# Finding the experts' indices by an exclusive or and a minimum instead of compare, multiply and sum

## The chip, the cores and the metric

The kernel runs on one core of a Trainium2 chip. The metric is the device time of one execution in microseconds (us), as the median of several runs. The core's engines are TensorE (PE in the profile, its weight loads PEld), VectorE (DVE), ScalarE (ACT), GpSimd (POOL) and SyncE (SP). Each works through a queue of its own in order; semaphores tie the queues together.

## The reference, cut to what matters

The whole computation is a block with two feed-forward layers and a mixer, and then two "hybrid" layers, each followed by a layer of many small experts (`peer_ffn`). For each of 256 tokens and 8 heads, that layer scores two lists of 128 keys, keeps the 16 best of each, adds them to 256 pairs, keeps the 16 best pairs, and needs the number of the expert behind each kept pair:

```python
def peer_ffn(x, w_query, sub_keys, down, up):
    q = (xt @ w_query).reshape(T, H, 2, PEER_HALF)
    s = jnp.einsum('thcd,cnd->thcn', q, sub_keys).astype(jnp.float32)
    sv, si = lax.top_k(s, K)                                    # K = 16, values and indices
    cand_s = (sv[:, :, 0, :, None] + sv[:, :, 1, None, :]).reshape(T, H, K * K)
    cand_i = (si[:, :, 0, :, None] * PEER_NKEYS + si[:, :, 1, None, :]).reshape(T, H, K * K)
    top_s, pos = lax.top_k(cand_s, K)                           # pos = 16 a + b
    idx = jnp.take_along_axis(cand_i, pos, axis=-1)             # the look-up
    gate = jax.nn.softmax(top_s, axis=-1)
    ...                                                         # sum of gate * gelu(down[idx] . x) * up[idx]
```

The change is in the look-up: from pos = 16 a + b to the a-th index of the first list and the b-th of the second.

## The kernel before, in words

Everything is a stream of weight tiles of 128x1024 float32, 512 KB each. A product in near float32 precision is made of three fast ones (`mm3`, L607 to L609): each weight tile is split into a high part (ScalarE, L1213) and a low part (the tile less its high part: VectorE, L1846, or GpSimd, L2720). There are four buffers for tiles as loaded and three for the parts, so the high part of tile k waits for TensorE to be through with tile k - 3, and TensorE waits for the low part of tile k before tile k. `LOWS` says which engine makes the low part. In an expert layer, with its tiles counted from 0, tiles 11 to 72 go three times to GpSimd and then once to VectorE: VectorE's are tiles 14, 18, 22, ..., 34, ..., 58, 62, 66, 70.

In an expert layer 8 tiles give the queries, 128 the scores of all 16384 experts (`down`), and 128 the sum (`up`). The kernel computes all experts and multiplies by gates that are zero except for the found ones. While tiles 8 to 67 are multiplied, VectorE searches beside its low parts. `BESIDE` spreads this `search` over 60 steps, one behind each tile, 30 for each half of the tokens (t = 0, 1). Each engine has a generator of its own; one `yield` is one step. Counted within a half (step 0 is at tile 8, or at tile 38), VectorE does: steps 1 to 11 the 16 best of each list (`best_of_keys`); step 12 the sum of pairs `cand` (L2564) and the conversion of the found indices to float, `sif` (L2567); steps 13 to 20 the 16 best pairs (L2575 to L2589); step 20, too, the shift, the mask and two conversions that give a and b (L2594 to L2599), and then the look-up of a half c = 0: compare (L2608, a 128x2048 one-hot of a against 0 to 15), step 21 multiply by the indices (L2612), step 22 sum over sixteen (L2615); steps 23 to 25 the same for c = 1; then the difference from the best (L2620), and after ScalarE's exponential (L1740) the gates (L2624 to L2628). TensorE turns the result at step 29 (L1159), and the one-hots of the next phase wait for it.

All eight PSUM banks are given out by `take` and `give` as a ring: the bank freed earliest is taken next, and TensorE waits in its queue for the event under which it was given. A pair of score tiles takes one bank, the keys' product (L1146) one, the turned result one.

Of the kernel before, what the change touches and what calls it, by code (L numbers as in the profile page):

```python
# [8 lines left out]
ALU = mybir.AluOpType  # L9
AX = mybir.AxisListType  # L10
F32 = mybir.dt.float32
F32R = mybir.dt.float32r
U32 = mybir.dt.uint32
# [338 lines left out]
def peer_memory(M, stage):  # L352
    m = Place()
    m.C = M.tensor(M.work_at, 128 * T).rearrange("p (n t) -> p n t", n=128)
    hole, M.hole = M.hole, None
    M.begin(M.work_at + 128 * T)
    m.keep = M.get3(3, T)
    m.temp = M.get3(2, T)
    m.waiting = [M.get3(8, 32) for _ in range(2)]
    M.hole = hole  # L360
    M.begin(M.work_at + 64 * T)
    m.qT, m.sk = M.get3(8, T), M.get(256)
    m.ws = [M.get(128) for _ in range(4)]
    m.sv, m.si, m.tv, m.pos = M.get(256), M.get(256), M.get(128), M.get(128)
    m.cand, m.eq, m.other = M.get(2048), M.get(2048), M.get(2048)
    m.sif, m.ab, m.out3 = M.get(256), M.get3(2, 128), M.get3(3, 128)
    assert M.at <= M.work_at + 128 * T
    M.hole = None
    M.begin(M.x_at)
    m.o1 = [M.get3(4, 128) for _ in range(2)]  # L370
    m.o2 = [M.get3(4, 128) for _ in range(2)]
    M.begin(M.x_at)
    m.his, m.los = [M.get3(4, T)], [M.get3(4, T)]
    M.begin(M.fixed_h)
    for ring in (m.his, m.los):
        ring += [M.get3(4, T) for _ in range(2)]
    M.hole = hole
    return m
# [208 lines left out]
class Tensor(Lane):  # L587
# [549 lines left out]
    def search(self):  # L1137
        M, m, e, s = self.M, self.m, self.e, self.s
        for t in range(2):
            for g in range(4):  # L1140
                bank = self.take()
                self.K.bank["keys", s, t, g] = bank
                self.wait_ge("peer_q", s, 3)
                self.wait_ge("sk_in", s)
                for i in range(2):
                    x = e.matmul(bank[:, 256 * i:256 * (i + 1)], m.qT[:, 2 * g + i, 128 * t:128 * (t + 1)], m.sk,  # L1146
                                 start=True, stop=True)
                x.then_inc(*self.S.tick("keys", s, t, g))
                yield
                yield  # L1150
                yield
                self.give(bank, ("keys_read", s, t, 2 * g + 1))
            for _ in range(17):
                yield
            bank = self.take()
            self.K.bank["found", s, t] = bank
            self.wait_ge("found", s, t, 2)
            for j in range(3):
                x = e.transpose(bank[:, 128 * j:128 * (j + 1)], m.out3[:, j], M.const("ident"))  # L1159
            x.then_inc(*self.S.tick("found_turned", s, t))  # L1160
            self.give(bank, ("kept", s, t))
            yield
# [674 lines left out]
class Vector(Lane):  # L1837
# [712 lines left out]

    def search(self):
        M, m, e, s = self.M, self.m, self.e, self.s
        iota16 = M.const("iota")[:, 0:16]
        e8, r8 = M.tiny(self.name, "e8", 8), M.tiny(self.name, "r8", 8)
        for t in range(2):
            for h in range(8):
                if h % 2 == 0:
                    yield
                self.best_of_keys(t, h)
                yield  # L2560
            s4 = m.sv.rearrange("p (h c k) -> p h c k", c=2, k=16)
            self.settle()
            self.wait_ge("keys_read", s, t, 7)
            e.tensor_tensor(m.cand.rearrange("p (h a b) -> p h a b", h=8, a=16),  # L2564
                            s4[:, :, 0].unsqueeze(3).to_broadcast([128, 8, 16, 16]),
                            s4[:, :, 1].unsqueeze(2).to_broadcast([128, 8, 16, 16]), ALU.add).then_inc(*self.mark())
            e.tensor_copy(m.sif, m.si.bitcast(U32)).then_inc(*self.mark())  # L2567
            yield
            for h0 in range(0, 8, 2):
                cs = [m.cand[:, 256 * h:256 * (h + 1)] for h in (h0, h0 + 1)]  # L2570
                v = [m.tv[:, 16 * h:16 * h + 16] for h in (h0, h0 + 1)]
                p = [m.pos[:, 16 * h:16 * h + 16].bitcast(U32) for h in (h0, h0 + 1)]
                self.settle()
                for i in range(2):
                    e.max(v[i][:, 0:8], cs[i]).then_inc(*self.mark())  # L2575
                first = self.n_own - 1
                for i in range(2):
                    self.settle(first + i)
                    e.max_index(p[i][:, 0:8], v[i][:, 0:8], cs[i]).then_inc(*self.mark())
                for i in range(2):  # L2580
                    self.settle(first + 2 + i)
                    e.match_replace(cs[i], v[i][:, 0:8], cs[i], TAKEN).then_inc(*self.mark())
                yield
                for i in range(2):
                    self.settle(first + 4 + i)
                    e.max(v[i][:, 8:16], cs[i]).then_inc(*self.mark())
                for i in range(2):
                    self.settle(first + 6 + i)
                    e.max_index(p[i][:, 8:16], v[i][:, 8:16], cs[i]).then_inc(*self.mark())  # L2589
                if h0 < 6:  # L2590
                    yield
            au, bu = m.eq[:, 0:128].bitcast(U32), m.eq[:, 128:256].bitcast(U32)
            self.settle()
            e.tensor_scalar(au, m.pos.bitcast(U32), 4, None, op0=ALU.logical_shift_right).then_inc(*self.mark())  # L2594
            e.tensor_scalar(bu, m.pos.bitcast(U32), 15, None, op0=ALU.bitwise_and).then_inc(*self.mark())
            self.settle(self.n_own - 1)
            e.tensor_copy(m.ab[:, 0], au).then_inc(*self.mark())
            self.settle(self.n_own - 1)
            e.tensor_copy(m.ab[:, 1], bu).then_inc(*self.mark())  # L2599
            s4f = m.sif.rearrange("p (h c k) -> p h c k", c=2, k=16)  # L2600
            if t:
                self.wait_ge("found_turned", s, 0)
            for c in range(2):
                buf = (m.eq, m.other)[c]
                b3 = buf.rearrange("p (k a) -> p k a", a=16)
                b4 = buf.rearrange("p (h k a) -> p h k a", h=8, a=16)
                self.settle()
                e.tensor_tensor(b3, iota16.unsqueeze(1).to_broadcast([128, 128, 16]),  # L2608
                                m.ab[:, c].unsqueeze(2).to_broadcast([128, 128, 16]), ALU.is_equal).then_inc(*self.mark())
                yield  # L2610
                self.settle()
                e.tensor_tensor(b4, b4, s4f[:, :, c].unsqueeze(2).to_broadcast([128, 8, 16, 16]), ALU.mult).then_inc(*self.mark())  # L2612
                yield
                self.settle()
                e.tensor_reduce(m.out3[:, 1 + c], b3, AX.X, ALU.add).then_inc(*self.S.tick("found", s, t, c))  # L2615
                if c == 0:
                    yield
            tv3 = m.tv.rearrange("p (h k) -> p h k", h=8)
            g3 = m.out3[:, 0].rearrange("p (h k) -> p h k", h=8)
            e.tensor_tensor(g3, tv3, tv3[:, :, 0:1].to_broadcast([128, 8, 16]), ALU.subtract).then_inc(*self.S.tick("best", s, t))  # L2620
            yield
            yield
            self.wait_ge("best_exp", s, t)
            e.tensor_reduce(e8, g3, AX.X, ALU.add).then_inc(*self.mark())  # L2624
            self.settle()
            e.reciprocal(r8, e8).then_inc(*self.mark())
            self.settle()
            e.tensor_tensor(g3, g3, r8.unsqueeze(2).to_broadcast([128, 8, 16]), ALU.mult).then_inc(*self.S.tick("found", s, t, 2))  # L2628
            yield
            yield  # L2630
            yield
# [609 lines left out]
```

## Time and profile before

| | us |
|---|---|
| median of 3 runs | 2531.29 |
| lowest, highest | 2525.47, 2531.94 |
| the profiled execution | 2531.54 |
| its span, first to last instruction | 2529.7 |
| TensorE busy | 2439.4 (96%) |
| VectorE busy | 1675.0 (66%) |
| ScalarE busy | 1204.4 (48%) |
| GpSimd busy | 711.8 (28%) |

Time in the rows below runs from the start of the span. "Busy" is the time in which an engine works on an instruction, or for VectorE and GpSimd also waits inside one for an access that it needs. The granted clock (PEclk) is the share of TensorE's full speed in a stretch; it has two levels, 1.2 and 2.4 GHz. Matmuls overlap, so the distance between two of them, which the chain of waits shows, says more than the length of one.

### The profile page before, as it was taken

What the parts mean: (1) busy time and instruction counts of PE and PEld (TensorE: products, weight loads), DVE (VectorE), ACT (ScalarE), POOL (GpSimd) and SP (SyncE); (2) the same over time, 40 slices, a digit from 0 to 9 for tenths busy, and PEclk for the clock granted to TensorE, in tenths of its full rate; (3) what the DMA queues carried; (4) which work ended last, traced back from release to release, by engine and by line L of the source; (5) the groups of instructions that cost most, each with busy time, mean ns of one, the idle gap of its engine ahead of it and who ended that gap; (6) DMA issues with size and microseconds to landing.
All of it is one profiled execution on the core that took longest, in us unless ns stands there. A gap on an engine that the chain in (4) does not pass through costs nothing.

```text
span 2529.7 us, 40330 instructions
## 1 busy us (share of the span) xinstructions
PE 2439.4 (96%) x16347; PEld 2233.2 (88%) x16347; DVE 1675.0 (66%) x3111; ACT 1204.4 (48%) x1827; POOL 711.8 (28%) x333
## 2 busy tenths in 40 slices
PE   4999899999999999999999999999999999999999
PEld 3997878988889999999888888889999999888887
DVE  6887775546565787899544445664877899644444
ACT  4444665445654444443444445654444444444443
POOL 3111001112025661000344443115663000244443
PEclk9999999999999999999999999999999999999999
DMA  7988444665345554444565665335554444555554
GB/s 282 327 300 308 162 138 151 216 195 171 109 159 170 169 166 154 139 142 142 191 196 192 194 193 194 127 125 186 165 177 157 137 140 142 181 192 193 193 192 165
DMA packets 126589, 457.45 MB, mean 181 GB/s; under 512 B 13974, under 2 KB 16962, under 8 KB 125635
## 3 DMA queue, kind: packets, MB, share of 16 engines
q1 hardware_dynamic: 121442, 441.52, 52.4%
q10 hardware_dynamic: 4048, 8.91, 1.0%
q0 software_dynamic: 912, 4.42, 0.5%
q8 instruction: 130, 2.13, 0.3%
q14 instruction: 57, 0.46, 0.1%
HBM read 451.62 MB, written 5.93 MB: 181 GB/s over the span
## 4 chain that ended last, share of the span: by engine, by line
PE 79%; DVE 6%; ACT 1%; issue 0%; POOL 0%; ACTq 0%; DVEq 0%; POOLq 0%
PE bank L607 24%; PE bank L609 23%; PE bank L608 23%; PE bank L1170 4%; DVE sb L2612 1%; DVE sb L2608 1%; DVE sb L1846 1%; PE bank L955 1%; PE bank L1146 1%; PE bank L816 0%; ACT sb L1213 0%; DVE sb L2615 0%; PE bank L622 0%; PE bank L1098 0%; PE bank L973 0%
## 5 line engine op out<-in xcount | busy, mean ns | idle before, releaser
L607 PE MATMUL bank<-sb,sb 128*128 128x256 f32 (+1 forms) x4744 | 1523.1, 321 | 49.1 <-DVE sb L1846 37.0
L608 PE MATMUL bank<-sb,sb 128*128 128x256 f32 (+1 forms) x4744 | 1497.3, 316 | 0.0
L609 PE MATMUL bank<-sb,sb 128*128 128x256 f32 (+1 forms) x4744 | 1497.2, 316 | 0.0
L1213 ACT ACTIVATE sb<-sb 128x1024 fp32r<-128x1024 f32 x765 | 806.6, 1058 | 1087.1 <-PE bank L609 1079.7
L2720 POOL TENSOR_TENSOR sb<-sb,sb 128x1024 fp32r<-128x1024 f32 x256 | 644.1, 2519 | 1337.6 <-ACT sb L1213 1333.6
L607 PEld LDWEIGHTS bank<-sb,sb 128*128 128x128 f32 x4744 | 911.5, 192 | 118.8 <-issue 35.4
L1846 DVE TENSOR_TENSOR sb<-sb,sb 128x1024 fp32r<-128x1024 f32 x509 | 626.2, 1231 | 559.6 <-ACT sb L1213 558.3
L608 PEld LDWEIGHTS bank<-sb,sb 128*128 128x128 f32 x4744 | 911.9, 192 | 55.2 <-issue 1.0
L609 PEld LDWEIGHTS bank<-sb,sb 128*128 128x128 f32 x4744 | 911.0, 192 | 55.4
L2684 DVE TENSOR_TENSOR sb<-sb,sb 128x1024 fp32r<-128x1024 f32 x64 | 160.0, 2499 | 149.7 <-ACT sb L1802 149.7
L2647 DVE TENSOR_SCALAR sb<-sb,sb 128x128 f32<-128x128 f32 x512 | 142.2, 341 | 0.0
L1170 PE MATMUL bank<-sb,sb 128*128 128x128 f32 x1024 | 135.3, 275 | 0.4 <-DVE sb L2647 0.4
L1170 PEld LDWEIGHTS bank<-sb,sb 128*128 128x128 f32 x1024 | 125.7, 192 | 0.7 <-issue 0.7
L1861 DVE CUSTOM_DVE_ANT_0 sb<-sb,sb 128x1024 f32<-128x1024 f32 x68 | 96.5, 1428 | 10.4 <-ACT sb L1219 5.8
L2643 DVE TENSOR_TENSOR sb<-sb,sb 128x512 f32<-128x512 f32 x128 | 87.3, 682 | 0.0
L2743 POOL TENSOR_TENSOR sb<-sb,sb 128x1 f32<-128x1 f32 (+2 forms) x28 | 18.6, 666 | 233.9 <-DVE sb L1882 101.0
L1802 ACT ACTIVATE sb<-sb 128x1024 fp32r<-128x1024 f32 x64 | 66.9, 1045 | 10.1 <-DVE sb L2679 5.1
L2658 DVE TENSOR_TENSOR sb<-bank,sb 128x288 f32<-128x288 f32 (+7 forms) x128 | 68.1, 534 | 0.0
L1362 ACT ACTIVATE sb<-sb 128x256 fp32r<-128x256 f32 x44 | 18.4, 418 | 102.4 <-DVE sb L2085 102.4
L622 PE MATMUL bank<-sb,sb 128*128 128x128 f32 x152 | 29.5, 336 | 32.0 <-DVE sb L1899 30.1
L622 PEld LDWEIGHTS bank<-sb,sb 128*128 128x128 f32 x152 | 21.4, 168 | 42.1 <-issue 28.4
L1780 ACT ACTIVATE sb<-bank 128x512 f32<-128x512 f32 (+7 forms) x120 | 57.7, 481 | 0.1
(274 smaller groups left out, 1238.7 us busy)
## 6 DMA issues: line engine op xcount, KB each, us to landing
sb<-in_peer_down_dram SPq DMA_DIRECT2D x256, 512.0 KB, 3.3
sb<-in_peer_up_dram SPq DMA_DIRECT2D x256, 512.0 KB, 3.3
sb<-in_w_ada_dram SPq DMA_DIRECT2D x72, 512.0 KB, 6.5
sb<-in_hyb_in_dram SPq DMA_DIRECT2D x56, 512.0 KB, 3.4
sb<-in_ffn_gate_dram SPq DMA_DIRECT2D x44, 512.0 KB, 4.3
sb<-in_ffn_up_dram SPq DMA_DIRECT2D x44, 512.0 KB, 5.2
sb<-in_ffn_down_dram SPq DMA_DIRECT2D x44, 512.0 KB, 4.3
sb<-in_mix_in_dram SPq DMA_DIRECT2D x25, 512.0 KB, 4.1
```

The source lines that it names most:

```text
L607: e.matmul(out, a[0], b[0], start=start, stop=False)
L608: e.matmul(out, a[0], b[1], start=False, stop=False)
L609: return e.matmul(out, a[1], b[0], start=False, stop=stop)
L1170: x = self.e.matmul(bank[:, 128 * j:128 * (j + 1)], m.o2[g % 2][:, j], m.o1[g % 2][:, j], start=True, stop=True)
L1213: self.e.activation(rr(M.hi[k % NSPLIT]), M.raw[k % NRAW], AF.Copy).then_inc(*self.S.tick("hi", k))
L1846: self.e.tensor_tensor(rr(M.lo[k % NSPLIT]), M.raw[k % NRAW], M.hi[k % NSPLIT], ALU.subtract).then_inc(*self.S.tick("lo_dve", k))
L1861: self.e.tensor_tensor_reduce(w, w, M.sc, 1.0, 0.0, ALU.mult, ALU.add, M.mod[:, o:o + 1]).then_inc(*self.S.tick("ada_dve", n))
L2643: e.tensor_tensor(o2, iota, m.keep[:, 2, 4 * g:4 * g + 4].unsqueeze(2).to_broadcast(wide), ALU.is_equal).then_inc(*self.S.tick("one_hot2", ...
L2647: x = e.tensor_scalar(o1[:, j], M.const("iota"), m.keep[:, 1, t:t + 1], m.keep[:, 0, t:t + 1], op0=ALU.is_equal, op1=ALU.mult)
L2658: e.tensor_tensor(c[:, 0:k], bank[:, 0:k], c[:, 0:k], ALU.mult).then_inc(*self.S.tick("gates_put", s, g))
L2684: self.e.tensor_tensor(rr(flat(m.los[i])), flat(m.C[:, 4 * n:4 * n + 4]), flat(m.his[i]), ALU.subtract).then_inc(*self.S.tick("up_lo", s, n))
L2720: self.e.tensor_tensor(rr(M.lo[k % NSPLIT]), M.raw[k % NRAW], M.hi[k % NSPLIT], ALU.subtract).then_inc(*self.S.tick("lo_pool", k))
```

## The change

Instead of a one-hot that is multiplied by the indices and summed, the kernel makes a table of 256 a + (the a-th index) as whole numbers. The found place gives 256 a of the pair wanted. An exclusive or of the two leaves the index alone where the a's agree, and something of at least 256 elsewhere; the smallest of the sixteen is the index. TensorE writes a (0 to 15, repeated for 8 heads and 2 lists) into a bank by a product with the identity, and VectorE multiplies by 256 and adds the indices within the bank. The number of steps stays 30 for each half of the tokens; the second minimum is at step 23, one step is empty, and the difference from the best stays at step 25.

```diff
@@ peer_memory
-    m.cand, m.eq, m.other = M.get(2048), M.get(2048), M.get(2048)
-    m.sif, m.ab, m.out3 = M.get(256), M.get3(2, 128), M.get3(3, 128)
+    m.cand = M.get(2048)
+    m.chosen = [M.get(2048).bitcast(U32) for _ in range(2)]
+    m.place, m.out3 = M.get3(2, 128).bitcast(U32), M.get3(3, 128)
@@ Tensor.search, after the four key products of a half (step 12)
+            bank = self.take()
+            self.K.bank["table", s, t] = bank
+            e.matmul(bank[:, 0:256], M.const("ident"), M.const("iota")[:, 0:16].unsqueeze(1).to_broadcast([128, 16, 16]),
+                     start=True, stop=True).then_inc(*self.S.tick("table", s, t))
+            self.give(bank, ("chosen", s, t, 1))
@@ Vector.search
-            e.tensor_copy(m.sif, m.si.bitcast(U32)).then_inc(*self.mark())
+            table = self.K.bank["table", s, t][:, 0:256]
+            self.wait_ge("table", s, t)
+            e.scalar_tensor_tensor(table.bitcast(U32), table, 256.0, m.si.bitcast(U32), ALU.mult, ALU.add).then_inc(*self.mark())
...
-            au, bu = m.eq[:, 0:128].bitcast(U32), m.eq[:, 128:256].bitcast(U32)
             self.settle()
-            e.tensor_scalar(au, m.pos.bitcast(U32), 4, None, op0=ALU.logical_shift_right).then_inc(*self.mark())
-            e.tensor_scalar(bu, m.pos.bitcast(U32), 15, None, op0=ALU.bitwise_and).then_inc(*self.mark())
-            self.settle(self.n_own - 1)
-            e.tensor_copy(m.ab[:, 0], au).then_inc(*self.mark())
-            self.settle(self.n_own - 1)
-            e.tensor_copy(m.ab[:, 1], bu).then_inc(*self.mark())
-            s4f = m.sif.rearrange("p (h c k) -> p h c k", c=2, k=16)
+            for c in range(2):
+                e.tensor_scalar(m.place[:, c], m.pos.bitcast(U32), (240, 15)[c], (4, 8)[c], op0=ALU.bitwise_and,
+                                op1=ALU.logical_shift_left).then_inc(*self.mark())
+            t4 = table.bitcast(U32).rearrange("p (h c a) -> p h c a", c=2, a=16)
             if t:
                 self.wait_ge("found_turned", s, 0)
             for c in range(2):
-                buf = (m.eq, m.other)[c]
-                b3 = buf.rearrange("p (k a) -> p k a", a=16)
-                b4 = buf.rearrange("p (h k a) -> p h k a", h=8, a=16)
                 self.settle()
-                e.tensor_tensor(b3, iota16.unsqueeze(1).to_broadcast([128, 128, 16]),
-                                m.ab[:, c].unsqueeze(2).to_broadcast([128, 128, 16]), ALU.is_equal).then_inc(*self.mark())
+                e.tensor_tensor(m.chosen[c].rearrange("p (h k a) -> p h k a", h=8, a=16),
+                                t4[:, :, c].unsqueeze(2).to_broadcast([128, 8, 16, 16]),
+                                m.place[:, c].rearrange("p (h k) -> p h k", h=8).unsqueeze(3).to_broadcast([128, 8, 16, 16]),
+                                ALU.bitwise_xor).then_inc(*self.S.tick("chosen", s, t, c))
                 yield
-                self.settle()
-                e.tensor_tensor(b4, b4, s4f[:, :, c].unsqueeze(2).to_broadcast([128, 8, 16, 16]), ALU.mult).then_inc(*self.mark())
+                self.wait_ge("chosen", s, t, c)
+                e.tensor_reduce(m.out3[:, 1 + c], m.chosen[c].rearrange("p (k a) -> p k a", a=16), AX.X, ALU.min).then_inc(
+                    *self.S.tick("found", s, t, c))
                 yield
-                self.settle()
-                e.tensor_reduce(m.out3[:, 1 + c], b3, AX.X, ALU.add).then_inc(*self.S.tick("found", s, t, c))
-                if c == 0:
-                    yield
+            yield
```

## Rows read from the trace of the kernel before

**Rows 1.** The page: busy time of each engine; the chain's shares.

```profile
PE 2439.4 (96%) x16347; PEld 2233.2 (88%) x16347; DVE 1675.0 (66%) x3111; ACT 1204.4 (48%) x1827; POOL 711.8 (28%) x333
...
PE 79%; DVE 6%; ACT 1%; issue 0%; POOL 0%; ACTq 0%; DVEq 0%; POOLq 0%
```

**Rows 2.** Busy time by stage: PE, PEld, DVE, ACT, POOL, clock, DMA share, GB/s.

```profile
760.00:970.00 210.00, 203.45 (x1644) 202.08 (x1643) 149.09 (x441) 94.08 (x109) 126.51 (x50) 0.98 0.51 168
```

**Rows 3.** TensorE's waits in the two search stretches: total us, times, longest us.

```profile
PE bank L607 <- DVE sb L1846: 6.5, 2, 4.2
...
PE bank L607 <- DVE sb L1846: 6.4, 2, 4.2
PE bank L1159 <- DVE sb L2628: 0.5, 1, 0.5
```

**Rows 4.** The chain that ended last around the first wait: start us, us, what.

```profile
835.84 0.14 DVE sb L2599
...
836.00 4.51 DVE sb L2608
...
840.54 4.39 DVE sb L2612
...
844.95 2.29 DVE sb L2615
847.24 1.14 DVE sb L1846
...
848.52 0.36 PE bank L607
...
849.53 0.21 PE bank L607
...
852.89 0.12 PE bank L608
```

**Rows 5.** The timeline of TensorE at the second and third wait.

```profile
950.59 0.36 PE L607 MATMUL bank<-sb,sb 128*128 128x256 f32 x1 [4.17 <-DVE sb L1846]
...
1815.92 0.36 PE L607 MATMUL bank<-sb,sb 128*128 128x256 f32 x1 [2.29 <-DVE sb L1846]
```

**Rows 6.** TensorE in stretches behind three waits: length, busy (count), granted clock, DMA.

```profile
850.00:852.00 2.00, 2.00 (x11) 0.50 1.01 403
1816.00:1820.00 4.00, 4.00 (x34) 1.00 0.81 288
1916.00:1920.00 4.00, 2.52 (x12) 0.71 0.35 123
```

**Rows 7.** The timeline of VectorE: the conversion, and a compare without GpSimd.

```profile
902.86 2.49 DVE L2567 CAST sb<-sb 128x256 f32<-128x256 uint32 x1
...
930.18 2.29 DVE L2608 TENSOR_TENSOR sb<-sb,sb 128x2048 f32<-128x2048 f32 x1
```

**Rows 8.** The timeline of GpSimd around the first wait.

```profile
835.96 2.40 POOL L2720 TENSOR_TENSOR sb<-sb,sb 128x1024 fp32r<-128x1024 f32 x1 [0.48 <-ACT sb L1213]
838.84 3.94 POOL L2720 TENSOR_TENSOR sb<-sb,sb 128x1024 fp32r<-128x1024 f32 x1 [0.48 <-ACT sb L1213]
```

**Rows 9.** VectorE's groups by form, mean ns of one: an operand in a bank.

```profile
L2658 DVE TENSOR_TENSOR sb<-bank,sb 128x480 f32<-128x480 f32 x16 | 10.1, 651 | 0.0
...
L2658 DVE TENSOR_TENSOR sb<-bank,sb 128x256 f32<-128x256 f32 x16 | 6.7, 418 | 0.0
```

**Rows 10.** The timelines of VectorE and GpSimd in the same time.

```profile
743.92 3.22 DVE L1948 SCALAR_TENSOR_TENSOR sb<-bank,sb,sb 128x256 fp32r<-128x256 f32 x8
...
742.95 5.66 POOL L2720 TENSOR_TENSOR sb<-sb,sb 128x1024 fp32r<-128x1024 f32 x2 [1.00 <-DVE sb L1899]
```

**Rows 11.** The timeline of ScalarE: two high parts that VectorE's low parts need.

```profile
840.58 1.06 ACT L1213 ACTIVATE sb<-sb 128x1024 fp32r<-128x1024 f32 x1 [1.82 <-PE bank L609]
...
940.44 1.06 ACT L1213 ACTIVATE sb<-sb 128x1024 fp32r<-128x1024 f32 x1 [1.81 <-PE bank L609]
```

**Rows 12.** The chain at one pair of key products.

```profile
770.85 0.86 PE bank L1146 x4
```

More of the change, by code:

```diff
@@ L2552, in search @@
         M, m, e, s = self.M, self.m, self.e, self.s
-        iota16 = M.const("iota")[:, 0:16]
         e8, r8 = M.tiny(self.name, "e8", 8), M.tiny(self.name, "r8", 8)
```

## The prediction

> **What bounds the kernel now.** I read the page first. TensorE is busy for 96% of the span and VectorE for 66%, and the chain that ended last runs through TensorE for 79% and through VectorE for 6% [rows 1]. So VectorE's time counts only where TensorE stands still for it. The table by stage gives the two stretches in which the search runs, one in each layer: of 210.00 us TensorE is busy 203.45 and VectorE 149.09 in the first [rows 2]. TensorE's waits in these two stretches name the rest: 6.5 us in two waits in the first layer and 6.4 us in two in the second, all before L607, for the subtraction L1846 (VectorE's low half of a weight tile), and 0.5 us for L2628 [rows 3].
>
> The chain through the first of these waits shows who was late. VectorE runs the compare L2608 for 4.51 us, the multiply L2612 for 4.39 and the sum L2615 for 2.29, and only then the low half L1846 that stands behind them in its queue. TensorE starts again at 848.52, and from about 849.5 to 852.7 its products come every 0.21 us, then every 0.12 again [rows 4]. The other waits look alike: TensorE starts again at 950.59 after 4.17 us and at 1815.92 after 2.29 [rows 5], and the longest of the second layer is again 4.2 us [rows 3]. The granted clock is at the lower of its two levels (0.50, which is 1.2 GHz of 2.4) after the first, above it and so partly low after the fourth (0.71), and stays at 1.00 after the third [rows 6].
>
> Why do compare and multiply take twice their time? L2608 took 2.29 us where it met no GpSimd work [rows 7] and 4.51 where it did [rows 4]. At 835.96 GpSimd had just begun a subtraction of 2.40 us, L2608 came at 836.00 and ended at 840.5; the next GpSimd subtraction came at 838.84 and took 3.94 [rows 8]. The two engines take turns, each waiting for the other's whole instruction, when VectorE reads two operands from SBUF.
>
> **What the four stalls cost now.** A wait costs its idle time, 0.24 us for a first product of 0.36 instead of 0.12 [rows 4], and the slow stretch. From 849.53 to 852.89 there are 16 products of 0.21 in 3.36 us, which at 0.12 would take 1.9: with the one that is slow in part, 1.5 us lost. I take the same after the second and the fourth wait. Hence:
> - first layer, t = 0: 2.29 + 0.24 + 1.5 = 4.0
> - first layer, t = 1: 4.17 + 0.24 + 1.5 = 5.9
> - second layer, t = 0: 2.29 + 0.24 = 2.5, with no slow clock
> - second layer, t = 1: 4.2 + 0.24 + 1.5 = 5.9
> - the wait of L1159 for L2628: 0.5
>
> Together 18.8 us, which is the most that the change can return.
>
> **The change, part by part.** *The chain of the look-up.* The compare and the multiply of each half go, and one exclusive or of 2048 elements takes their place, one operand of it in PSUM. Operations of this kind with one operand in a bank: 128x480 takes 651 ns and 128x256 takes 418, so 1.04 ns an element and, at 2048, 0.65 + 1568 x 0.00104 = 2.28 us [rows 9]. Does it wait for GpSimd? L1948, which reads a bank and one SBUF tensor, ran eight times in 3.22 us from 743.92, inside two GpSimd subtractions that held from 742.95 to 748.6 [rows 10]. It didn't wait, so I take 2.3 us. The upper bound is 4.5, a compare that takes turns. The minimum of sixteen takes the sum's place, with one input of the same shape: 2.29 [rows 4]; its input is uint32, as it was not before, and I give it no other price. Two conversions fall away, 0.14 us each [rows 4].
>
> *Time line at t = 0, first layer.* The two instructions for the places stand where the shift and the mask stood, with their shapes, and I give them the same time. Without the two conversions the first exclusive or starts at 835.7 instead of 836.0 [rows 4]; then 2.3 + 2.3 + 2.3 for or, minimum, or: 842.6. The high half that L1846 needs is there at 840.58 + 1.06 = 841.6 [rows 11]. L1846 takes 1.14 [rows 4] and ends at 843.8. TensorE wants it at 848.52 - 2.29 = 846.2. Margin 2.3 us, and the stall is gone.
>
> *At t = 1.* The first low half comes after the place instructions and the first compare, which already met no GpSimd work: 930.18 + 2.29 = 932.4 [rows 7], and with 1.14 for L1846 933.5. Here nearly nothing changes, and no wait of TensorE stands there today. After it now: 933.5 + 2.3 + 2.3 + 2.3 = 940.4 for minimum, or, minimum. The high half is there at 940.44 + 1.06 = 941.5 [rows 11], so L1846 ends at 942.7; TensorE wants it at 950.59 - 4.17 = 946.4. Margin 3.7 us. What is late next here is the high half itself, which waits for TensorE's own tile three back and leaves this margin. The second layer has the same lengths, so both its stalls go, and with VectorE some 7 us earlier L1159 no longer waits.
>
> *The table product.* TensorE gets four more products of 128x256 in plain float32 (two layers, two halves). Two such products, the keys' L1146, took 0.86 us [rows 12], so 0.43 each and 1.7 in all, on the path because TensorE is never idle there. The stationary operand is another and the moving one repeats its words; the bounds are 0 (no reason for a gain) and 2 x 0.43 = 0.86 each, 3.4 in all.
>
> *The table's instruction on VectorE* replaces the conversion L2567, which takes 2.49 us on 256 elements because it waits for GpSimd [rows 7]. A bank operand at 256 elements takes 0.42 [rows 9], so VectorE is 2 us earlier at this step, four times, all covered by TensorE's work. It brings a wait for the table product, with the whole selection of the 16 best and the next low half queued behind it. At t = 0 VectorE is at this step at 814.5, five us after TensorE has passed. At t = 1 it is close: TensorE wants tile 66 at 946.4, so at 2.88 us a tile (24 products of 0.12) tile 50 ends at 946.4 - 15 x 2.88 = 903.2, the table is ready at about 903.7, and VectorE came to L2567 at 902.86 [rows 7]. That wait of 0.8 us eats a part of the 2 us just won, so it costs nothing.
>
> *The bank.* The table holds one of eight banks from step 12 until the second exclusive or. Banks are taken in turn, and the seventh take after it is the pair of tiles 34 and 35 (t = 0) or 64 and 65 (t = 1). At t = 0 the second or ends at 842.6, before tile 34 is wanted at 846.2; at t = 1 it ends at 938.1, and tile 64 starts at 946.4 - 2 x 2.88 = 940.6. Margin 2.6 us, no wait.
>
> **Sum.** 18.8 - 1.7 = 17.1 us. The profiled execution took 2531.5 us (span 2529.7), which is the median of the runs shown (2531.3) to 0.3. 2531.5 - 17.1 = 2514.4, against the median 2514.2; I say 2514.
>
> **A rule that speaks against it.** L2608 reads a word repeated sixteen times and a row of sixteen words, and ran at 1.12 ns an element [rows 7]. The Trainium skill, "Vector Engine (DVE) Microarchitecture Reference", section 5.2, says that a port keeps its full rate only for runs of two or more adjacent words, and gives 1.73 ns a column for an exclusive or one of whose sources hops at every element. By it the exclusive or, if a repeated word counted as a hop, would take 3.5 us (an estimate from that page). The trace doesn't agree for repeated words in a compare.
>
> **The rivals.** Let D be the time of the exclusive or. From the two time lines the t = 0 stall is 2(D - 3.5), and the low half at t = 1 is late by D - 3.6 (tile 62 is wanted at 946.4 - 4 x 2.88 = 934.9).
> - *Integer operands lose the 1.04 ns rate mildly*, D = 3.5, as it would where repeated words are slow. For it: no uint32 pair with a bank operand in the trace. Against it: [rows 7]. Each half stalls for a few tenths, which costs 0.3 + 0.24, with the slow clock up to 1.5 more: 2516 to 2521. Chance 5%.
> - *The exclusive or takes turns with GpSimd after all*, D = 4.4. Stalls of 1.9 at t = 0, 0.8 at t = 1 before tile 62, and 0.8 before tile 64, where TensorE waits for the bank; with 0.24 each and one or two slow stretches 6 us a layer, 12 in all: 2514.4 + 12 = 2526. Against it stands [rows 10]. Chance 6%.
> - *The clock doesn't come back*: TensorE is no longer idle but the slow stretches stay, 3 x 1.5 = 4.5 us: 2519. For it: the clock stayed high after the third stall, so idleness alone doesn't set it. Against it: the slow products begin within a us or so of a restart [rows 4]. Chance 5%.
> - *Slower.* The bitwise operation on 32-bit integers from PSUM needs several cycles an element. From D = 5.0 the stalls (3.0 at t = 0, 1.4 before tile 62, 1.5 before tile 64 for the bank, 0.24 each, two slow stretches: 9.6 a layer) and the table products exceed the 18.8 us of now; at 6.7 us, three times the rate of [rows 9], t = 0 stalls for 6.4, t = 1 for 3.1 and again 3.1, with clock some 17 a layer: 2514.4 + 34 = 2548. Nothing in the trace shows such an operation at such a rate. Chance 3%.
>
> **How the numbers follow.** The forecast, all stalls gone at 2514, gets 81%. Its own range is -2 (the clock after the fourth stall, the keys' stretch with less work before it) to +4 (the table product at 0.86, a stall left over of some tenths), plus what three runs of before differ, 6 us: 2508 to 2521. The second and the fourth of the cases lie in this, too; up to 2522 about 1 in 10 is left out. Faster by over 0.3% (7.6 us, about what a measurement of this kernel can tell from no change) means below 2523.7: 0.88. Within: 0.08, mainly the second rival. Slower: 0.04.
>
> **What would show it.** In the profile after: no wait of L607 for L1846 in the two search stretches, and none of L1159; the exclusive or x8 at 2.3 us with minimum, median and maximum alike; GpSimd's subtractions of 3.94 back at 2.40; the granted clock of both stretches at 1.00; four table products at 0.43. VectorE's busy time falls: eight compares and eight multiplies of 2.3 to 4.5 leave, eight of 2.3 come. A third of the gain missing with the clock low would show the third rival; a wait of L607 for ScalarE's Gelu or for the or itself would show that the bank is late. I am wrong if D is above 3.5.

## The result

| | before | after |
|---|---|---|
| median of 4 runs, us | 2531.09 | 2512.03 |
| lowest to highest | 2525.47 to 2531.94 | 2509.72 to 2513.0 |
| span of the profiled execution | 2529.7 | 2510.7 |
| TensorE's waits of L607 (L608 after) for VectorE's low half, whole span | 37.0 us, 18 times | 23.7 us, 14 times |

The ratio is 0.9928 with a 95% interval of 0.9916 to 0.9940: 19 us or 0.72% faster. Lines have moved by one to six: the three products are now L608 to L610, VectorE's low half L1852, ScalarE's high half L1219, the one-hots' product L1176; GpSimd's low half is still L2720.

The page of the changed kernel, busy time and the chain's shares, which answer to [rows 1]:

```profile
PE 2432.4 (97%) x16355; PEld 2228.2 (89%) x16355; DVE 1623.3 (65%) x3095; ACT 1206.1 (48%) x1827; POOL 697.0 (28%) x333
...
PE 83%; DVE 2%; ACT 1%; issue 0%; POOL 0%; ACTq 0%; POOLq 0%
```

VectorE's share of the chain fell from 6% to 2%, and its busy time by 52 us. Its share of the span was, as before, not the point. The table by stage (length; PE, PEld, DVE, ACT and POOL busy; clock, DMA share, GB/s), against [rows 2]:

```profile
770.00:960.00 190.00, 190.00 (x1558) 189.04 (x1557) 120.23 (x430) 89.80 (x103) 117.07 (x48) 1.00 0.54 174
1728.00:1917.00 189.00, 189.00 (x1551) 188.04 (x1550) 119.69 (x429) 89.80 (x103) 116.59 (x48) 1.00 0.54 174
```

In both search stretches TensorE is busy all the time and the granted clock is 1.00. The stretch of [rows 2] is 20 us longer; in 770 to 960 alone, the kernel before had TensorE busy for 183.45 us and VectorE for 142.69. The list of TensorE's waits in these stretches is empty, where [rows 3] had 6.5 and 6.4 us and the 0.5 us of L1159.

VectorE's timeline at the look-up of t = 0 in the first layer, against the chain of [rows 4]:

```profile
835.22 0.61 DVE L2601 TENSOR_SCALAR sb<-sb 128x128 uint32<-128x128 uint32 x2
835.87 2.29 DVE L2608 TENSOR_TENSOR sb<-bank,sb 128x2048 uint32<-128x2048 uint32 x1
838.20 2.29 DVE L2614 TENSOR_REDUCE sb<-sb 128x128 f32<-128x2048 uint32 x1
840.40 2.28 DVE L2608 TENSOR_TENSOR sb<-bank,sb 128x2048 uint32<-128x2048 uint32 x1
842.60 1.22 DVE L1852 TENSOR_TENSOR sb<-sb,sb 128x1024 fp32r<-128x1024 f32 x1
843.73 2.28 DVE L2614 TENSOR_REDUCE sb<-sb 128x128 f32<-128x2048 uint32 x1
```

And GpSimd's in the same time, against [rows 8]:

```profile
836.09 2.41 POOL L2720 TENSOR_TENSOR sb<-sb,sb 128x1024 fp32r<-128x1024 f32 x1 [0.47 <-ACT sb L1219]
838.97 2.41 POOL L2720 TENSOR_TENSOR sb<-sb,sb 128x1024 fp32r<-128x1024 f32 x1 [0.47 <-ACT sb L1219]
```

The second exclusive or starts at 840.40, while GpSimd is at work from 838.97 to 841.38, and takes 2.28 us. GpSimd's subtractions take 2.41 both times, where the second took 3.94, though the first exclusive or ran from 835.87 to 838.16. The low half starts at 842.60 instead of 847.24.

The instructions by line, for the exclusive or and for the table's instruction (durations in ns: shortest, median, longest):

```profile
L2608 DVE TENSOR_TENSOR sb<-bank,sb x8: 2280/2288/2293, 835.9 to 1889.6; 128x2048 uint32<-128x2048 uint32 x8
...
L2574 DVE SCALAR_TENSOR_TENSOR bank<-bank,sb x4: 420/426/433, 814.2 to 1857.1; 128x256 uint32<-128x256 f32 x4
...
  PE bank L1156: 0.9, 2
```

The exclusive or took 2280 to 2293 ns in all eight cases. The table's instruction took 0.42 us instead of 2.49, and had to wait for the table product in two of the four cases, 0.9 us together. One table product on the chain:

```profile
808.50 0.43 PE bank L1156 x2
```

A measure that leaves out the rest of the kernel is the time from the first key product to the first one-hots' product of a layer. The view of a single line gives the first and the last start (after the durations); for the two lines in the first layer of the changed kernel:

```profile
L1147 PE MATMUL bank<-sb,sb x32: 377/378/379, 770.4 to 890.0; 128*128 128x256 f32 x32
...
L1176 PE MATMUL bank<-sb,sb x512: 272/275/348, 960.1 to 1195.8; 128*128 128x128 f32 x171
```

Before, the lines were L1146 and L1170. The differences of the first starts:

| | first layer | second layer |
|---|---|---|
| before | 969.7 - 770.7 = 199.0 | 1936.7 - 1738.1 = 198.6 |
| after | 960.1 - 770.4 = 189.7 | 1917.7 - 1728.0 = 189.7 |

18.2 us of the 19.0 by which the spans differ are here. I call it the search time below.

### The profile page after: what moved, and what is told of

It reads as the page before. It is cut to its first block, busy times and chain, and to the rows that moved or that the text cites. A ratio compares the mean times of both kernels' runs of the same rounds, so it can differ in the third digit from the quotient of the medians.

```text
span 2510.7 us, 40330 instructions
## 1 busy us (share of the span) xinstructions
PE 2432.4 (97%) x16355; PEld 2228.2 (89%) x16355; DVE 1623.3 (65%) x3095; ACT 1206.1 (48%) x1827; POOL 697.0 (28%) x333
## 4 chain that ended last, share of the span: by engine, by line
PE 83%; DVE 2%; ACT 1%; issue 0%; POOL 0%; ACTq 0%; POOLq 0%
PE bank L608 25%; PE bank L609 25%; PE bank L610 25%; PE bank L1176 4%; PE bank L956 1%; PE bank L1147 1%; PE bank L817 1%; DVE sb L1852 0%; PE bank L1099 0%; PE bank L623 0%; PE bank L974 0%; POOL sb L2743 0%; DVE sb L1905 0%; PE bank L806 0%; PE bank L1061 0%
## 5 line engine op out<-in xcount | busy, mean ns | idle before, releaser
L608 PE MATMUL bank<-sb,sb 128*128 128x256 f32 (+1 forms) x4744 | 1520.5, 321 | 36.5 <-DVE sb L1852 23.7
L610 PE MATMUL bank<-sb,sb 128*128 128x256 f32 (+1 forms) x4744 | 1493.9, 315 | 0.0
L1219 ACT ACTIVATE sb<-sb 128x1024 fp32r<-128x1024 f32 x765 | 808.1, 1060 | 1085.2 <-PE bank L610 1077.2
L1852 DVE TENSOR_TENSOR sb<-sb,sb 128x1024 fp32r<-128x1024 f32 x509 | 625.2, 1229 | 585.1 <-ACT sb L1219 583.8
L608 PEld LDWEIGHTS bank<-sb,sb 128*128 128x128 f32 x4744 | 907.9, 191 | 104.6 <-issue 20.9
L2720 POOL TENSOR_TENSOR sb<-sb,sb 128x1024 fp32r<-128x1024 f32 x256 | 629.3, 2460 | 1336.6 <-ACT sb L1219 1332.6
L610 PEld LDWEIGHTS bank<-sb,sb 128*128 128x128 f32 x4744 | 907.8, 191 | 55.9
L1176 PE MATMUL bank<-sb,sb 128*128 128x128 f32 x1024 | 135.3, 275 | 0.4 <-DVE sb L2647 0.4
L1176 PEld LDWEIGHTS bank<-sb,sb 128*128 128x128 f32 x1024 | 125.7, 192 | 0.7 <-issue 0.7
```

Of the source, the lines that this page charges most:

```text
L608: e.matmul(out, a[0], b[0], start=start, stop=False)
L610: return e.matmul(out, a[1], b[0], start=False, stop=stop)
L1176: x = self.e.matmul(bank[:, 128 * j:128 * (j + 1)], m.o2[g % 2][:, j], m.o1[g % 2][:, j], start=True, stop=True)
L1219: self.e.activation(rr(M.hi[k % NSPLIT]), M.raw[k % NRAW], AF.Copy).then_inc(*self.S.tick("hi", k))
L1852: self.e.tensor_tensor(rr(M.lo[k % NSPLIT]), M.raw[k % NRAW], M.hi[k % NSPLIT], ALU.subtract).then_inc(*self.S.tick("lo_dve", k))
L2720: self.e.tensor_tensor(rr(M.lo[k % NSPLIT]), M.raw[k % NRAW], M.hi[k % NSPLIT], ALU.subtract).then_inc(*self.S.tick("lo_pool", k))
```

## The experiments

Is it that the operand left SBUF, or that one pass over 2048 elements fell away? Two kernels do one of the two alone.

**One operand in PSUM, all three passes kept.** The kernel before, with:

```diff
@@ Tensor.search, step 12: the table product of the change
@@ Vector.search
-            e.tensor_copy(m.sif, m.si.bitcast(U32)).then_inc(*self.mark())
...
+            e.tensor_copy(bank[:, 256:512], m.si.bitcast(U32)).then_inc(*self.mark())
...
-            s4f = m.sif.rearrange("p (h c k) -> p h c k", c=2, k=16)
+            s4f = bank[:, 256:512].rearrange("p (h c k) -> p h c k", c=2, k=16)
...
-                e.tensor_tensor(b3, iota16.unsqueeze(1)
...
+                e.tensor_tensor(b3, bank[:, 0:16].unsqueeze(1)
...
```

The bank is free again when the second multiply (c = 1) has read it, where the changed kernel frees it after the second exclusive or.

> The kernel before with its compare, multiply and sum kept; only one operand of the compare (0 to 15) and one of the multiply (the indices as floats) lie in a PSUM bank, written by the same table product and one conversion. Theory (the operand out of SBUF ends the turns with GpSimd): all three instructions take 2.29 us; at t = 0 the low half ends at 836.0 + 3 x 2.3 + 1.14 = 844.0 where TensorE wants it at 846.2, at t = 1 at 933.5 + 4 x 2.3 + 1.14 = 943.9 against 946.4. No wait of TensorE for the low half in either search, 2512 to 2514 us: the whole gain without one pass fewer. Rival (what counts is the pass that falls away): the stalls of 2.3 and 4.2 us stay, and the time is 2531 + 1.7 = 2533.

Measured: 2524.68 us, ratio 0.9979 (0.9969 to 0.9988), search time 198.0 in both layers. Neither theory had that. The traced execution is one of the slower of the ten (2528.81 us, where the lowest is 2522.46), so its search times show less of a gain than the median does; the last section says what these executions differ in. TensorE's waits in the first search (total us, times, longest):

```profile
PE bank L607 <- DVE sb L2618: 4.8, 2, 2.4
```

TensorE waits for L2618, the multiply, and not for the low half. VectorE's and TensorE's timelines around the first wait:

```profile
835.82 2.29 DVE L2614 TENSOR_TENSOR sb<-bank,sb 128x2048 f32<-128x2048 f32 x1
838.15 2.29 DVE L2618 TENSOR_TENSOR sb<-sb,bank 128x2048 f32<-128x2048 f32 x1
840.47 2.29 DVE L2621 TENSOR_REDUCE sb<-sb 128x128 f32<-128x2048 f32 x1
842.67 1.22 DVE L1851 TENSOR_TENSOR sb<-sb,sb 128x1024 fp32r<-128x1024 f32 x1
843.80 2.28 DVE L2614 TENSOR_TENSOR sb<-bank,sb 128x2048 f32<-128x2048 f32 x1
846.12 2.29 DVE L2618 TENSOR_TENSOR sb<-sb,bank 128x2048 f32<-128x2048 f32 x1
```

```profile
848.46 0.38 PE L607 MATMUL bank<-sb,sb 128*128 128x256 f32 x1 [2.41 <-DVE sb L2618]
```

Compare, multiply and sum take 2.29 us each and the low half of tile 34 is done at 843.8, as the theory had it (844.0). But TensorE wants the bank again at 846.05. The second multiply, which reads it last, ends at 848.4. The rule of the bank (the seventh take is tile 34) stands in the prediction, and I had not applied it to this kernel.

**The same, with the bank taken six steps later.**

```diff
@@ Tensor.search
+            for _ in range(6):
+                yield
             bank = self.take()
...
-            for _ in range(17):
+            for _ in range(11):
                 yield
@@ Vector.search: the conversion into the bank moved from step 12 to step 20
```

> As e1_psum_operands, but TensorE takes the bank and makes the table product six steps later, and VectorE converts the indices into it right before the first compare. Theory (in e1 the stalls of 2.4 us are not the look-up's length but the bank: TensorE wants it at tile 34 and 64, before the second multiply has read it): the seventh take now falls at tile 40 and 70, the two waits of 4.8 us in each search are gone, and the time is that of the changed kernel, 2512 to 2514, with compare, multiply and sum all kept. Rival (one pass fewer is what brings it): a wait of TensorE of 1 us or more stays in each half, 2518 or more.

Measured: 2513.30 us, ratio 0.9938 (0.9921 to 0.9955), search time 189.8 and 189.7, as in the changed kernel. TensorE waits for nothing in either search. TensorE in the first search stretch (length, busy, clock), then compare and multiply by line:

```profile
772.00:961.00 189.00, 189.00 (x1551) 1.00 0.53 174
...
L2616 DVE TENSOR_TENSOR sb<-bank,sb x8: 2282/2288/2292, 837.8 to 1894.2; 128x2048 f32<-128x2048 f32 x8
...
L2620 DVE TENSOR_TENSOR sb<-sb,bank x8: 2281/2286/2289, 840.1 to 1896.5; 128x2048 f32<-128x2048 f32 x8
```

So with all three passes kept, an operand in PSUM brings the whole gain. The fewer passes are not needed for it. What they do need is a bank that nobody wants early.

**The exclusive or with its table in SBUF.** The changed kernel, with:

```diff
-    m.place, m.out3 = M.get3(2, 128).bitcast(U32), M.get3(3, 128)
+    m.place, m.out3, m.table = M.get3(2, 128).bitcast(U32), M.get3(3, 128), M.get(256)
...
-            e.scalar_tensor_tensor(table.bitcast(U32), table, 256.0, m.si.bitcast(U32), ALU.mult, ALU.add).then_inc(*self.mark())
+            e.scalar_tensor_tensor(m.table.bitcast(U32), table, 256.0, m.si.bitcast(U32), ALU.mult, ALU.add).then_inc(*self.mark())
...
-            t4 = table.bitcast(U32).rearrange("p (h c a) -> p h c a", c=2, a=16)
+            t4 = m.table.bitcast(U32).rearrange("p (h c a) -> p h c a", c=2, a=16)
```

> The changed kernel, but the table of 256 a + index is written to SBUF, so the exclusive or reads two operands from SBUF. Theory (turns come back, but one pass fewer leaves room for them): the exclusive or takes 2.3 where it comes first and up to 4.5 where GpSimd does, and some of GpSimd's subtractions take about 4 instead of 2.4; at t = 0 the low half comes at 844 to 846.5 against 846.2, so TensorE waits for 0 to 0.5 us in each layer, 2512 to 2517 us. Rival (the turns alone made the stalls): an exclusive or of 4.4 each time, 6 us lost a layer, 2524. Rival (the turns have nothing to do with it): 2.3 each time and GpSimd at 2.40.

Measured: 2513.55 us, ratio 0.9935 (0.9920 to 0.9950), search time 191.5 and 191.6, 1.8 to 1.9 more than with the table in PSUM. TensorE's wait, then GpSimd's and VectorE's timelines:

```profile
PE bank L608 <- POOL sb L2720: 1.3, 1, 1.3
...
832.99 12.17 POOL L2720 TENSOR_TENSOR sb<-sb,sb 128x1024 fp32r<-128x1024 f32 x3 [0.48 <-ACT sb L1219]
...
832.77 2.29 DVE L2608 TENSOR_TENSOR sb<-sb,sb 128x2048 uint32<-128x2048 uint32 x1
...
839.50 3.39 DVE L1852 TENSOR_TENSOR sb<-sb,sb 128x1024 fp32r<-128x1024 f32 x1
```

The turns are back, and VectorE comes first: the exclusive or takes 2.29 us, the three subtractions of GpSimd take 12.17 together where 7.2 would do, and the low half of VectorE itself takes 3.39 instead of 1.22. TensorE waits 1.29 us, this time for GpSimd's low half. I had expected at most 0.5 us, and at VectorE's. So the shorter look-up with the turns back still brings 7.5 and 7.0 us of the 9.3 and 8.9. This holds for the order in which the two engines come here: the exclusive or took 2280 to 2322 ns in all eight cases, so it never had to wait for GpSimd to speak of, and in this one it came first by 0.22 us. The two conversions that fell away, 0.27 us together, are enough to give it this lead; in the kernel before, GpSimd was first by 0.04 us [rows 8]. What the exclusive or would cost where GpSimd comes first was not run.

**The table product four times** (three more `e.matmul` into the same bank before the one that is there).

> The changed kernel with the table product made four times instead of once, 12 products of 128x256 float32 more. Theory (each lies on TensorE's path at 0.43 us): +5.2 us on the changed kernel, 2517.2. Rival (a product is hidden somewhere): 2512. At the upper bound of 0.86 each it would be 2522.

Measured: 2516.67 us, ratio 0.9948 (0.9932 to 0.9963); search time 192.3 and 192.2, 2.6 and 2.5 more for six products: 0.43 each. The chain at one table:

```profile
808.02 1.30 PE bank L1157 x6
809.32 0.43 PE bank L1159 x2
```

1.73 us for four products. Each lies on the path at its full length.

**Without the table product.** VectorE writes the table from 0 to 15 and the indices, and waits itself for the bank:

```diff
@@ Tensor.search
-            bank = self.take()
-            e.matmul(bank[:, 0:256], M.const("ident"), M.const("iota")[:, 0:16].unsqueeze(1).to_broadcast([128, 16, 16]),
-                     start=True, stop=True).then_inc(*self.S.tick("table", s, t))
+            bank, self.K.bank["table_free", s, t] = self.free.pop(0)
             self.K.bank["table", s, t] = bank
@@ Vector.search
-            self.wait_ge("table", s, t)
-            e.scalar_tensor_tensor(table.bitcast(U32), table, 256.0, m.si.bitcast(U32), ALU.mult, ALU.add).then_inc(*self.mark())
+            for event in self.K.bank["table_free", s, t]:
+                self.wait_ge(*event)
+            e.scalar_tensor_tensor(table.bitcast(U32).rearrange("p (r a) -> p r a", a=16),
+                                   M.const("iota")[:, 0:16].unsqueeze(1).to_broadcast([128, 16, 16]), 256.0,
+                                   m.si.bitcast(U32).rearrange("p (r a) -> p r a", a=16), ALU.mult, ALU.add).then_inc(*self.mark())
```

> The changed kernel without the table product: VectorE writes the table into the bank itself from 0 to 15 and the indices, both in SBUF, and waits itself for the event under which the bank was freed. Theory: TensorE saves 4 x 0.43 = 1.7 us, VectorE's instruction takes 2.5 us where it meets GpSimd, as the conversion before the change did, and has room for it: 2510.3 us, no new wait of TensorE. Rival: the longer instruction or the earlier bank makes a low half late, 2512 or more.

Measured: 2509.84 us, ratio 0.9918 (0.9904 to 0.9931), search time 188.8 in both layers, 0.9 less each. The table's instruction by line:

```profile
L2573 DVE SCALAR_TENSOR_TENSOR bank<-sb,sb x4: 2630/2632/2632, 813.2 to 1854.2; 128x256 uint32<-128x256 f32 x4
```

It reads two operands from SBUF and takes 2.63 us each time, but has room. Since 2.2 us between two medians is less than these runs can tell, both kernels ran again, side by side on one chip.

> The changed kernel once more, unaltered, on the same chip as the next one, so that the two can be set side by side. Theory: 0.992 to 0.994 of the kernel before, no wait of TensorE of over 0.3 us in either search.

Measured: 2508.09 us, ratio 0.9916 (0.9902 to 0.9929), search time 189.7 and 189.7.

> The version without the table product again, beside the changed kernel. Theory: 1.7 us (0.07%) less than the changed kernel, four products of 0.43 us; the intervals of the two will overlap, and the spans between the first key product and the first gate product are the sharper measure: 0.9 us less in each layer. Rival: the 2.2 us seen between the medians was noise and VectorE's longer table instruction takes it back: no less.

Measured: 2511.87 us, ratio 0.9927 (0.9914 to 0.9941), search time 188.8 and 188.9. The order of the medians is the other way round. The 0.9 us is there in both layers of both pairs of traces; in the whole time it can't be told from noise, so this version is not shown to beat the changed kernel. Both beat the kernel before.

**The bank held too long.** The changed kernel with two more minima at t = 1, before the first one (step 21):

```diff
                 self.wait_ge("chosen", s, t, c)
+                for _ in range(2 if t == 1 and c == 0 else 0):
+                    e.tensor_reduce(m.ws[0], m.chosen[c].rearrange("p (k a) -> p k a", a=16), AX.X, ALU.min).then_inc(*self.mark())
+                    self.settle()
                 e.tensor_reduce(m.out3[:, 1 + c], ...)
```

> The changed kernel with two more minima of 2.29 us before the first one at t = 1 (step 21), so that the second exclusive or ends at 934.3 + 4.6 = 938.9, while TensorE wants tile 64 at 936.9. Theory (the bank is the seventh take): TensorE waits 2.1 us for the exclusive or itself in each layer, and the low half of tile 66, at 942.4, is in time for a TensorE that is now at 945; 2.1 + 0.24 and 0 or 1.5 of slow clock a layer: 5 to 8 us above the changed kernel. Rival (the bank is not wanted then): no such wait, and TensorE waits for nothing.

Measured: 2517.44 us in one run; search time 193.5 and 192.1, that is 3.8 and 2.4 more. TensorE's timeline at the wait:

```profile
937.76 0.39 PE L608 MATMUL bank<-sb,sb 128*128 128x256 f32 x1 [2.08 <-DVE sb L2608]
```

2.08 us for the exclusive or, once in each layer, 2.1 expected (the 1.4 between the layers is the clock, below), and no wait for the low half of tile 66. So the margin of the bank in the changed kernel is real: the exclusive or ends at 934.3 and TensorE takes the bank at 936.9.

**Two more minima at t = 0**, behind the second exclusive or (step 22).

```diff
                                 ALU.bitwise_xor).then_inc(*self.S.tick("chosen", s, t, c))
+                if c == 1 and t == 0:
+                    self.wait_ge("chosen", s, t, c)
+                    for _ in range(2):
+                        e.tensor_reduce(m.ws[0], m.chosen[c].rearrange("p (k a) -> p k a", a=16), AX.X, ALU.min).then_inc(*self.mark())
+                        self.settle()
```

> The changed kernel with two more minima behind the second exclusive or at t = 0 alone (step 22): the low half of tile 34 starts at 842.6 + 4.6 = 847.2 instead of 842.6 and is done at 848.5, and TensorE wants it at 846.2. Theory (a margin of 2.3 us): a wait for VectorE's low half of 2.2 to 2.4 us in each layer, as in the kernel before, and a loss of 2.5 to 4.0 a layer, 5 to 8 in all. Rival (a stall costs only its idle time): 4.6 in all.

Measured: 2518.85 us in one run; search time 192.3 and 192.4, that is 2.6 and 2.7 more than in the changed kernel. TensorE's timeline:

```profile
849.83 0.35 PE L608 MATMUL bank<-sb,sb 128*128 128x256 f32 x1 [2.36 <-DVE sb L1852]
```

2.36 us of waiting and 2.6 in all in a layer: as expected, at the lower end, since the clock stayed high.

**One more minimum in both halves** (the same, with `if c == 1` and `range(1)`).

> The changed kernel with one more minimum behind the second exclusive or in both halves (step 22): the low half of tile 34 is done at 846.2, just when TensorE wants it. Theory (margins of 2.3 us at t = 0 and over 3 at t = 1): waits of at most 0.2 us, time within 1 us of the changed kernel, 2512 to 2513. Rival (no such margin): waits of over 1 us and 4 us or more.

Measured: 2517.05 us in one run; search time 191.9 and 192.0. TensorE waits 1.97 us for the low half in each layer, where at most 0.2 us and a time of 2512 to 2513 us were expected. VectorE's and GpSimd's timelines:

```profile
842.78 2.29 DVE L2615 TENSOR_REDUCE sb<-sb 128x128 f32<-128x2048 uint32 x1
845.10 3.16 DVE L1852 TENSOR_TENSOR sb<-sb,sb 128x1024 fp32r<-128x1024 f32 x1
...
844.79 2.38 POOL L2725 TENSOR_TENSOR sb<-sb,sb 128x1024 fp32r<-128x1024 f32 x1 [3.35 <-ACT sb L1219]
```

The low half came at 845.10 and took 3.16 us instead of 1.22, because it reads two operands from SBUF and GpSimd had begun at 844.79. A margin of 2.3 us for its end was the wrong account: its start has to come before GpSimd's. In the changed kernel it starts at 842.60 and GpSimd at 844.73, so a delay of more than 2.1 us crosses this line and costs two at once.

## Why the prediction was right

2514 us was forecast and 2512.03 measured; the range was 2508 to 2522.

- *What bounds the kernel*: right. The four stalls before the low half and the one of L1159 are gone, and nothing took their place.
- *The time line at t = 0*: exclusive or at 835.7, ends at 838.0, 840.3 and 842.6 forecast; 835.87, and the next instructions at 838.20, 840.40 and 842.60 measured.
- *The time line at t = 1* is the forecast one, 3.8 us earlier, since TensorE comes earlier:

```profile
926.48 2.29 DVE L2608 TENSOR_TENSOR sb<-bank,sb 128x2048 uint32<-128x2048 uint32 x1
928.69 1.22 DVE L1852 TENSOR_TENSOR sb<-sb,sb 128x1024 fp32r<-128x1024 f32 x1
929.82 2.28 DVE L2614 TENSOR_REDUCE sb<-sb 128x128 f32<-128x2048 uint32 x1
932.02 2.28 DVE L2608 TENSOR_TENSOR sb<-bank,sb 128x2048 uint32<-128x2048 uint32 x1
934.33 2.29 DVE L2614 TENSOR_REDUCE sb<-sb 128x128 f32<-128x2048 uint32 x1
938.11 1.23 DVE L1852 TENSOR_TENSOR sb<-sb,sb 128x1024 fp32r<-128x1024 f32 x1 [1.49 <-ACT sb L1219]
```

  The low half waits for ScalarE there, which I had named as next late.
- *The exclusive or*: 2.28 from the slope over elements, 2.29 measured; that it doesn't wait for GpSimd was read from the one kind of instruction that had run beside it [rows 10]. The minimum over uint32 took 2.28.
- *The table product*: 0.43 each, shown by making it four times. *The table's instruction* had a wait of 0.8 us forecast at t = 1 in each layer; it was 0.45.
- *The bank*: no wait here, and two kernels that hold it for longer wait at just this take, so the count of seven takes was right.
- *The sum*: 17.1 us forecast, 19.1 between the medians, 19.0 between the spans, 18.2 in the two searches. For the first layer 9.9 - 0.86 = 9.0 was forecast and 9.3 came; for the second 8.9 - 0.86 = 8.0, and 8.9 came. The term that was sized too small is thus the loss in the second layer, by 0.9 us, and 18.8 us was not the most that the change could return: without the table products' 1.7, the two searches would have become 19.9 us shorter. The trace of the kernel before shows most of the rest. TensorE stood still briefly at three more places, once in the first layer and twice in the second:

```profile
940.44 0.35 PE L607 MATMUL bank<-sb,sb 128*128 128x256 f32 x1
...
1824.82 0.39 PE L607 MATMUL bank<-sb,sb 128*128 128x256 f32 x1
...
1907.34 0.35 PE L607 MATMUL bank<-sb,sb 128*128 128x256 f32 x1
```

  The products before these start at 940.07, 1824.51 and 1906.97, so 0.31 to 0.37 us lie between two products instead of 0.12, and up to 0.1 more behind each: some 0.3 us each time, 0.6 in the second layer. The profile names no releaser for so short a wait, but a GpSimd subtraction that took turns and ran for 4.49 us from 1820.28 ended at 1824.77, just before the second of them: the turns made GpSimd's low halves late, too. For L1159, 0.80 us lie between its start and that of the product before it, and I had given its wait 0.5 us and no restart: 0.2 more. The last 0.8 us lie outside the searches, where two traces of one kernel differ as much (2510.7 and 2509.8 us of the changed kernel, with equal search times).
- *The slow clock*: 4.5 us of the 18.8 are three slow stretches of one execution of the kernel before. By the last section the clock fell behind half of the waits of 2.0 to 2.4 us, so the two stalls of 2.29 us could have had two slow stretches, or none, in another execution. That one of each came, and an execution near the median, is luck in the hit.
- *The reason for the gain*: half right. The prediction put it to a look-up of two passes that doesn't take turns. The runs show that either alone brings all or most of the gain: three passes without turns give 189.7 to 189.8 us of search time, two passes with turns, in which VectorE came first, 191.5 and 191.6, both together 189.7. The prediction also tied the turns to two operands from SBUF, although its own row of the conversion L2567 has one and 2.49 us [rows 7].
- *The rivals*: none came, and the granted clock came back to 1.00 in both searches. The exclusive or keeps the rate of [rows 9] for whole numbers and for words repeated sixteen times. The rule of the Trainium skill ("Vector Engine (DVE) Microarchitecture Reference", section 5.2) on single hopping words does not reach to repeated ones here: 1.12 ns an element. But the rivals' prices were off: an exclusive or of 3.5 us would start the low half at 845.0, and by the run with one more minimum that costs about 2 us a layer, not 0.5. The threshold I gave was for the end of an instruction that itself has to take turns.

## What to carry to other kernels

Where VectorE and GpSimd both read two operands from SBUF, each waits for the whole of the other's instruction. One operand in PSUM ended that here: three passes without turns had a search time 1.7 to 1.9 us shorter than two with them. Two kinds of VectorE instruction behave otherwise. The conversion of 256 indices waited with only one operand, 2.49 us from SBUF to SBUF, and took 0.42 with its output in PSUM (the run with one operand in PSUM: at 813.89, with GpSimd at work from 812.73 to 818.61). The sum and the minimum over sixteen, which read one operand, took 2.27 to 2.29 us in all cases, also beside GpSimd. Count a held bank in takes, not in time: find which instruction takes it next and check that against the last reader, for every version. A margin in front of an instruction that takes turns ends where the other engine's next instruction starts, not where its own result is due.

## What the runs showed of the hardware

TensorE's clock after a wait of about 2 us is not set by the length of the wait alone. TensorE in stretches of 4 us behind four waits (length, busy, clock, DMA): first behind 2.41 us in the kernel with one operand in PSUM and the bank held,

```profile
849.00:853.00 4.00, 4.00 (x23) 0.59 0.53 181
```

then behind 2.36 us in the kernel with two more minima,

```profile
850.00:854.00 4.00, 4.00 (x35) 1.00 0.83 294
```

then behind the two waits of 2.08 us of one and the same execution of the kernel with the bank held too long, one in each layer:

```profile
938.00:942.00 4.00, 4.00 (x24) 0.61 0.29 113
1900.00:1904.00 4.00, 4.00 (x35) 1.00 0.21 57
```

Over all traces with a wait of 1.97 to 2.41 us in the searches the clock fell to its lower level behind 6 of 12 (before 1 of 2, three passes with the bank held 4 of 4, bank late 1 of 2, one more 0 of 2, two more 0 of 2). Behind 4.2 us it fell in 2 of 2, behind 1.3 us in 0 of 2. Where it fell (0.50 in between, 1.2 GHz), 4 us held 23 or 24 products instead of 35 or 36, so it costs about 1.5 us. What decides in between is open. Whole executions of one kernel differ in the clock, too, there in all stretches and not the searches alone. Of seven of the kernel before on one chip the shortest, 2523.34 us, had a mean granted clock of 0.996 and the longest, 2531.76, one of 0.991. Of the ten of the kernel with one operand in PSUM, the three with 0.995 took 2522.46 to 2522.81 us and the four with 0.991 took 2527.01 to 2529.84; of the five of the changed kernel run again, the three with 0.997 took 2506.51 to 2508.09 and the one with 0.992 took 2513.21.
